# Two chunks of the modulation vector: row blocks summed on VectorE, then one sum over partitions on TensorE, in the first feed-forward network of a two-block model

## What is computed

```python
mod_lat = jnp.split(jax.nn.silu(c) @ w_ada[l] + b_ada[l], 6, axis=-1)
mod_ctx = jnp.split(jax.nn.silu(c_ctx)[None, :] @ w_ada[l] + b_ada[l], 6, axis=-1)
sh1, sc1, gt1, sh2, sc2, gt2 = mod_lat
sh1c, sc1c, gt1c, sh2c, sc2c, gt2c = mod_ctx
```

```python
(jax.nn.silu(h @ w_gate) * (h @ w_up)) @ w_down
```

## Time and profile before

| | |
|---|---|
| median of three runs | 2476.98 us (2474.41 to 2478.2) |
| profiled execution | 2477.59 us |
| its span, first to last instruction | 2475.8 us |
| TensorE busy | 2287.5 us, 92% |
| VectorE busy | 1066.9 us, 43% |
| ScalarE busy | 843.8 us, 34% |
[...]

### The profile page before, as it was taken

The page is one execution under the profiler, slowest core; times in us unless marked ns, Lnnn a source line. Parts: engine busy times, 40 slices in busy tenths (PEclk is TensorE's granted clock), DMA queues, the critical chain, the costliest instruction groups (busy, mean ns, idle before and its releaser), DMA issues.

```text
span 2475.8 us, 29368 instructions
## 1 busy us (share of the span) xinstructions
PE 2287.5 (92%) x11126; PEld 1741.5 (70%) x11126; DVE 1066.9 (43%) x1591; ACT 843.8 (34%) x1288; POOL 39.7 (2%) x29
## 2 busy tenths in 40 slices
PE   4588899999998789999999999998999998999997
PEld 2354667777866556888888766666888876888885
DVE  4685343323346664534334344444433334333332
ACT  4332332222235464433223344333222223222222
POOL 3200000000000000000000000000000000000000
PEclk9698899999999899999999999989999999999998
DMA  6589545545422003233233211111333322332331
GB/s 187 192 272 306 199 136 181 179 149 186 141 76 69 9 18 95 71 109 104 83 106 115 70 51 52 51 40 47 88 100 93 93 85 68 93 111 85 94 106 55
DMA packets 360892, 269.98 MB, mean 109 GB/s; under 512 B 20402, under 2 KB 346400, under 8 KB 350544
## 3 DMA queue, kind: packets, MB, share of 16 engines
q1 hardware_dynamic: 346928, 256.37, 33.8%
q10 hardware_dynamic: 13856, 12.13, 1.9%
HBM read 265.39 MB, written 3.08 MB: 108 GB/s over the span
## 4 chain that ended last, share of the span: by engine, by line
PE 80%; DVE 7%; ACT 4%; DVEq 2%; issue 2%; DMA 2%; POOLq 2%; ACTq 1%; SPq 0%; POOL 0%
PE G L482 58%; PE G L1921 8%; PE AD L394 2%; DVE tb L562 1%; PE MS L1257 1%; PE MS L2150 1%; PE X L2131 1%; PE X L2397 1%; ACT whi L462 1%; PE X L1663 1%; DVE wlo L468 1%; DVEq L561 1%; PE X L1627 1%; DMA TTall<-blocks 0%; PE G L1123 0%
## 5 line engine op out<-in xcount | busy, mean ns | idle before, releaser
L468 DVE TENSOR_TENSOR wlo<-raw,whi 128x1024 fp32r<-128x1024 f32 (+1 forms) x296 | 380.8, 1287 | 1010.0 <-ACT whi L462 1009.0
L462 ACT ACTIVATE whi<-raw 128x1024 fp32r<-128x1024 f32 (+1 forms) x296 | 328.1, 1108 | 940.7 <-PE G L482 778.7
L482 PE MATMUL G<-Ahi,whi 128*128 128x512 f32 x1440 | 574.8, 399 | 17.0 <-DVE Alo L567 9.7
L482 PE MATMUL G<-Ahi,wlo 128*128 128x512 f32 x1440 | 563.6, 391 | 0.0
L482 PE MATMUL G<-Alo,whi 128*128 128x512 f32 x1440 | 563.6, 391 | 0.0
L482 PEld LDWEIGHTS G<-Ahi,whi 128*128 128x128 f32 x1440 | 272.3, 189 | 99.2 <-issue 30.6
L482 PEld LDWEIGHTS G<-Ahi,wlo 128*128 128x128 f32 x1440 | 272.6, 189 | 58.2 <-issue 3.4
L482 PEld LDWEIGHTS G<-Alo,whi 128*128 128x128 f32 x1440 | 272.2, 189 | 57.8
L482 PE MATMUL G<-mhi,whi 128*128 128x512 f32 x528 | 212.0, 402 | 0.0
L482 PE MATMUL G<-mlo,whi 128*128 128x512 f32 x528 | 205.7, 390 | 0.0
L482 PE MATMUL G<-mhi,wlo 128*128 128x512 f32 x528 | 205.5, 389 | 0.0
(11 more groups left out here) (503 smaller groups left out, 2673.1 us busy)
## 6 DMA issues: line engine op xcount, KB each, us to landing
ada_s<-in_ada_w SPq DMA_DIRECT2D x48, 1024.0 KB, 7.5
raw<-in_w_in SPq DMA_DIRECT2D x64, 512.0 KB, 4.1
ada_ff<-in_w_ada SPq DMA_DIRECT2D x24, 1024.0 KB, 6.1
raw<-in_ffn_w_gate SPq DMA_DIRECT2D x44, 512.0 KB, 3.9
raw<-in_ffn_w_up SPq DMA_DIRECT2D x44, 512.0 KB, 3.9
raw<-in_ffn_w_down SPq DMA_DIRECT2D x32, 704.0 KB, 4.7
raw<-in_w_ffn_in SPq DMA_DIRECT2D x44, 512.0 KB, 3.9
raw<-in_w_ffn_out SPq DMA_DIRECT2D x16, 704.0 KB, 4.7
```

The costliest lines, as they stand in the source:

```text
L462: last = E.eng.activation(whi[j][:, k0:k0 + k, 0:c], raw[j][:, k0:k0 + k, 0:c], ACT.Copy)
L468: last = E.eng.tensor_tensor(wlo[j][:, k0:k0 + k, 0:c], raw[j][:, k0:k0 + k, 0:c], whi[j][:, k0:k0 + k, 0:c].bitcast(FP32), ALU.subtract)
L482: mm = E.eng.matmul(out_, a[j][:, k0 + kk, 0:c], b(kk), start=first and kk == 0 and n == 0, stop=last and kk == k - 1 and n == 2)
```

## The change

Chunks 7 and 8 of the modulation (16 slices) leave TensorE. VectorE scales each row block by its conditioning value, which differs by partition, and adds it to a new tile `ada_sum` (128 x 2048): `late_sum_dve`, a tensor_scalar for the first block of a chunk and a scalar_tensor_tensor for the seven others. Then `late_sum_pe` sums over the partitions with four matmuls of a column of ones, into the same rows of `AD`. The passes stand in VectorE's hooks: slices 8 to 15 behind pairs 3 to 10 of gu0, 16 to 18 behind pairs 1 to 3 of dn0, 19 to 23 behind pairs 0 to 4 of gu1. The two sums on TensorE are behind pair 0 of dn0 and pair 6 of gu1. Eviction and transposes of chunk 8 move one pair back in gu1, and slices 24 and 25 from pairs 7 and 8 to 8 and 9. The order of the chunks of `w_ada_2` becomes 1, 2, 0, so that the chunk with two conditioning columns is chunk 9 and stays on TensorE; its bias is added for both in the latent stage.

```diff
+        ada_sum = sb("ada_sum", [P, 2 * D], where=ff)
...
-                ("ff", A["kv_ada_w"], 0, 1), ("ff", A["w_ada_2"][0], 0, 2), ("ff", A["w_ada_2"][0], 1, 1),
-                ("ff", A["w_ada_2"][0], 2, 1)])
+                ("ff", A["kv_ada_w"], 0, 1), ("ff", A["w_ada_2"][0], 1, 1), ("ff", A["w_ada_2"][0], 2, 1),
+                ("ff", A["w_ada_2"][0], 0, 2)])
...
             if k == 0:
                 E.eng.wait_ge(S("ada_taken"), c + 1)
+                if s:
+                    E.eng.wait_ge(S("late_done"), s)
...
+        def late_sum_dve(E, s):
+
+            c, k, j = 6 + s // KD, s % KD, s % NSLOT
+            if k == 0:
+                E.eng.wait_ge(S("late_done"), s)
+                if c == 8:
+                    E.eng.wait_ge(S("ada_summed"), 1)
+            E.eng.wait_ge(S(f"dma_l{j}"), 16 * (s // NSLOT + 1))
+            scale = cact[:, KD + k:KD + k + 1]
+            if k == 0:
+                E.eng.tensor_scalar(ada_sum[:, :], ada_ff[j][:, :], scale, None, ALU.mult)
+            else:
+                E.eng.scalar_tensor_tensor(ada_sum[:, :], ada_ff[j][:, :], scale, ada_sum[:, :], ALU.mult, ALU.add)
+            E.eng.drain().then_inc(S("late_done"), 1)
+
+        def late_sum_pe(E, c):
+
+            E.eng.wait_ge(S("ada_taken"), c + 1)
+            E.eng.wait_ge(S("late_done"), KD * (c - 5))
+            for b in range(4):
+                mm = E.eng.matmul(AD[32 * b:32 * b + 1, :], ones[:, 0:1], ada_sum[:, b * 512:(b + 1) * 512],
+                                  start=True, stop=True)
+            mm.then_inc(S("ada_summed"), 1)
...
+            elif c in (7, 8):
+                E.eng.wait_ge(S("ada_summed"), c - 6)
...
-                o = 16 * (c - 7)
+                o = (16, 32, 0)[c - 7]
                 add(modb[:, o:o + 16, 0], 0, V_ADAB + o)
-                if c == 7:
+                if c == 9:
                     add(modb[:, 0:16, 1], 1, V_ADAB)
...
         def ffn_hooks_pe(E, ph):
             if ph == "gu0":
-                return {1: lambda: late_slice(E, 6), 2: lambda: late_slice(E, 7), 3: lambda: ada_turn(E, 6),
-                        **{i: lambda s=4 + i: late_slice(E, s) for i in range(4, 11)}}
+                return {1: lambda: late_slice(E, 6), 2: lambda: late_slice(E, 7), 3: lambda: ada_turn(E, 6)}
             if ph == "dn0":
-                return {0: lambda: late_slice(E, 15), 1: lambda: ada_turn(E, 7), 2: lambda: late_slice(E, 16),
-                        3: lambda: late_slice(E, 17)}
+                return {0: lambda: late_sum_pe(E, 7), 1: lambda: ada_turn(E, 7)}
             if ph == "gu1":
-                return {**{i: lambda s=18 + i: late_slice(E, s) for i in range(6)}, 6: lambda: ada_turn(E, 8),
-                        7: lambda: late_slice(E, 24), 8: lambda: late_slice(E, 25)}
+                return {6: lambda: late_sum_pe(E, 8), 7: lambda: ada_turn(E, 8),
+                        8: lambda: late_slice(E, 24), 9: lambda: late_slice(E, 25)}
...
-                i, c = {"gu0": (2, 6), "dn0": (0, 7), "gu1": (5, 8)}[ph]
+                i, c = {"gu0": (2, 6), "dn0": (0, 7), "gu1": (6, 8)}[ph]
...
-                i, c = {"gu0": (3, 6), "dn0": (1, 7), "gu1": (6, 8)}[ph]
-                return {i: lambda: ada_take(E, c)}
+                sums = {"gu0": {i: 5 + i for i in range(3, 11)}, "dn0": {i: 15 + i for i in range(1, 4)},
+                        "gu1": {i: 19 + i for i in range(5)}}[ph]
+                i, c = {"gu0": (3, 6), "dn0": (1, 7), "gu1": (7, 8)}[ph]
+
+                def hook(n):
+                    if n == i:
+                        ada_take(E, c)
+                    if n in sums:
+                        late_sum_dve(E, sums[n])
+                return {n: lambda n=n: hook(n) for n in {i, *sums}}
```

## The result

The changed kernel takes 2456.44 us (median of four runs, 2455.39 to 2458.16), the kernel before beside it 2477.59 us (2474.41 to 2479.38). The ratio is 0.9911, with a 95% interval of 0.9891 to 0.993: faster by 0.7 to 1.1%. The forecast was 2460.5 us, with a range from 2457 to 2465. The measured median lies 4.1 us under the forecast and 0.6 us under the low end of the range.

What follows compares the result with a forecast made beforehand. TensorE, busy 92% of the span, was taken as the bound. Removing 19.2 us and adding 2.4 nets -16.8 us: 2460.8 from the profiled run, 2460.2 from the median, forecast 2460.5 us, range 2457 to 2465.

Steps and rivals of the forecast that it cites:

- the sum: Whole kernel: the profiled time of before, 2477.59 us, less the net 16.8 us on TensorE, gives 2460.8 us.
- Removed, 16 x 1.20 us: First feed-forward network: 16 slices leave TensorE's hooks, each costing 1.20 us on the path, 19.2 us in all.
- Added, two sums at 1.20 each: TensorE in the first feed-forward network: two sums over partitions, priced like a slice, add 2.4 us.
- The pass at 2.38 us: VectorE, end of a pair: each of 16 passes over 128x2048 f32 takes 2.38 us, at most 3.01.
- The cover of 5.06 us: Gu pairs: VectorE's idle gap of 1.94 us plus 3.12 us spare before the next tile is needed hides a pass.
- That VectorE becomes the bound: Rival, chance 0.04: a VectorE pass takes far over 2.38 us; at 6.4 us the kernel is slower, 2482 us.
- The down tile at +8.1 us: Start of dn1: the tile lands 8.1 us after tile 19 of gu1 ends, 0.7 us short of a stall.
- the forecast's 0: Start of dn1: TensorE's stall from SP's later loads was taken as 0 us, between bounds of 0 and 3.4.
- The clock rival: Rival, chance 0.06: work behind the change, now earlier, meets low-clock stretches otherwise; 2456.5 to 2464.5 us.
- That the change doesn't do what it says: Rival, chance 0.04: TensorE's slices only filled idle time, which now appears as waits; 2472 to 2481 us.

Runs made afterwards that it cites:

- the doubled kernel: The changed kernel with each of its 14 scalar_tensor_tensor passes on VectorE made twice: 2459.93 us, ratio 0.9934 to the kernel before.

## Why the prediction fell short: its steps, one by one

**What failed is the sum**, "2477.59 - 16.8 = 2460.8". Its only term was the network. It had none for the end stage, where the change takes another 2.1 us, because in the shorter program the instruction load that lay on the first output store comes some 14 us ahead of it. With it the sum is 2477.59 - 16.9 - 2.1 = 2458.6 us, from the median 2458.0, inside the range. The forecast's own list of what could move stages outside the change named only the clock.

The second part of the miss is the low end of the range. All runs of the study together are 14 of the changed kernel (mean 2457.4, standard deviation 1.9) and 82 of the kernel before (mean 2477.2, 2.3): a difference of 19.8 us, give or take 1.1 (1.96 times the root of 1.9 x 1.9 / 14 + 2.3 x 2.3 / 82). Shown by stage are 16.9 + 2.1 = 19.0 us. The 0.8 us between is within the error. The two medians of the result are 21.15 us apart, 1.35 more than that, which is the scatter of four runs on each side; the mean of the 14, 2457.4, lies inside the range. A low end at 2457.0 left 3.5 us for everything that had no term, and 2.1 of it were taken.

**Removed, 16 x 1.20 us: right.** Putting 14 such groups back cost 1.21 us each. Part of what a slice costs beyond its own piece stands in the timeline of the kernel before, 396 to 400 us: the first product behind the slice takes 0.50 us where the others take 0.39 or 0.40, and the next one starts 0.34 us after it instead of 0.23. **Added, two sums at 1.20 each: right**, with the piece of 0.97 us in the chain; the network is shorter by 16.87 us where 16.8 was said.

**The pass at 2.38 us: right**, measured 2.346. VectorE's next work followed 0.13 us behind its end: the pass began at 408.84 and ended at 411.18, `wlo` began at 411.31, and three passes with a drain between them took 7.20 us.

**The cover of 5.06 us: right in place, its edge less sharp.** 4.78 us cost 0.14 us a pair, 7.20 us cost 1.57 instead of the 2.14 that lie over the cover. That VectorE becomes the bound was a real rival in its mechanism; tripled passes show it. The pass's length kept it away.

**The down tile at +8.1 us, trusted least: right in its verdict, short in its size.** Its rounding could start at +8.6; the margin was 0.2 us and not 0.7. SP's issue came at +1.4 rather than +1.65, but the landing took 7.2 us after it and not 6.45. Load 31 landed 5.1 us after its own issue, 2.5 us ahead of the tile. With slice 25 one pair later, and in the doubled kernel, the load landed 5.0 us after its issue, 2.5 and 3.0 us ahead of the tile. So in all three the tile landed behind the whole of the load; whether the load holds it back, or the two only share the transfer, no run shows. One pair later the stall is 10.74 us, and in the doubled kernel, where the tile took 7.6 us, TensorE stood still at this place for 0.2 us: that the forecast's 0 held in the changed kernel was in part luck.

**The clock rival** was that the work behind the change, now 16.8 us earlier, meets the stretches of low granted clock otherwise. In the one of 830 to 840 us TensorE was busy for 8.04 us at 0.52, so some 4 us either way by the author's estimate. That gave 2456.5 to 2464.5, whose edge the result meets, but not by its mechanism: filling TensorE late instead of early left the middle stage alone (1734.8 and 1734.9 us), and by means 0.1 us is left for it, give or take 1.5. That the change doesn't do what it says is excluded by the network's 16.87 us.

**What stays open.** That the instruction load on the first store belongs to TensorE's program follows from the edits: the runs that edited VectorE's hooks alone kept the 72 or 73 loads of their base and the length of its end stage, those that added matmuls to TensorE's moved or added loads; the trace does not name its owner. Why that load slows a store of the output by 2.2 us was not tried. The 0.8 us beyond the shown parts may be chance or a small effect on the middle stage. One rival for them stands untested: the kernel before with passes was 2.1 us faster by means, and the changed kernel without them 1.2 us slower, both outside the network.

## What to carry to other kernels

Work on the path is priced by the difference of two pairs of the trace, with and without it, and not by its own record (1.20 against 0.97 us); an engine half idle on average takes over such work free as long as the operation and its lateness together stay under the spare time of the next buffer, here 5 us a pair. A hook that is moved by one place takes SP's queue with it: look at what is queued behind the load that it releases, since here one more place turned 0.2 us of margin into 13.3 us lost. And leave the range a few us for stages that the edit does not touch: compare start, middle and end stage over several executions before a residue gets a reason.

## What the runs showed of the hardware

- The length of the end stage goes with the place of an instruction load of 16 KB. 56 tiny matmuls in the first network moved it onto the first output store of the changed kernel and off that of the kernel before. In all 14 profiles the store takes 4.2 to 4.4 us and the stage 24.4 to 24.6 with such a load in the last 16 us, 2.0 and 22.3 to 22.4 without.
- Four matmuls of one column by one column cost 0.38 us on the path ((373.93 - 368.60) / 14), against 1.21 for one column by 512. Put beside a slice in the kernel before, the same four cost 0.07 us ((386.48 - 385.47) / 14).
- After 10.74 us without work (slice 25 later) the granted TensorE clock was 0.50 for the next 3.3 us, and 1.00 from 653 us on, some 6 us after TensorE had begun again.
- A 704 KB tile issued 0.4 us behind a load of 1 MB landed after 7.1, 7.2 and 7.6 us in three kernels, against a median of 4.7 over all such tiles; the load in front landed 2.5, 2.5 and 3.0 us before it.
